# A hybrid decoder step on one core: the prompt's eight tiles in parts of 1, 2, 2, 2, 1 in place of 2, 2, 2, 2

## The reference, cut to what matters

```python
def layer(x, ...):
    n1 = rmsnorm(x, norm1_g)
    proj = n1 @ w_in          # q,k,v of attention; q,k,v,gates of GLA; merge gates ga, gb
    oa = banded_swa(qa, ka, va, attn_sinks)         # window of 128, 16 heads, 4 KV heads
    og, S_new = gla_recurrent(qg, kg, vg, log_a, S0, ...)   # state runs over the tokens, 4 heads
    og = rmsnorm(og, gla_norm_g) * silu(rb)
    u = sigmoid(ga) * oa + sigmoid(gb) * og
    x = x + u @ w_out
    return x + peer(rmsnorm(x, norm2_g), ...), new_k, new_v, S_new

def peer(h, ...):             # 8 heads, 16 experts each: 128 of 16384 experts for every token
    q = xk @ peer_wq          # 1024 -> 2048
    ... top 16 of 128 keys in two halves, top 16 of their sums, softmax -> eidx, g
    ue = take(peer_u, eidx)   # a row of 1024 floats for each token and expert
    act = gelu(sum(ue * xk))
    ve = take(peer_v, eidx)
    return sum(g * act * ve)
```

## Time and profile before

| | us |
|---|---|
| median of 3 runs (3849.88 to 3872.11) | 3852.84 |
| the profiled execution | 3859.83 |
| its span, first to last instruction | 3858.0 |
| indices of the first tile ready | 484.2 |
| indices of the first tile of parts 1, 2, 3 ready | 1216.0, 2165.3, 3010.2 |

### The profile page before, as it was taken

How to read it: one execution, slowest core, us unless ns; L and a number is a source line. 1 busy time by engine, 2 the same in 40 slices (tenths; PEclk the granted TensorE clock), 3 DMA queues, 4 the chain that set the end, 5 groups by cost and what they waited for, 6 DMA issues and landing times.

```text
span 3858.0 us, 33048 instructions
## 1 busy us (share of the span) xinstructions
PE 2894.0 (75%) x10008; PEld 1798.1 (47%) x10008; DVE 2808.5 (73%) x5630; ACT 731.2 (19%) x1677; POOL 2443.4 (63%) x2076
## 2 busy tenths in 40 slices
PE   8778689888687997887988768878777555555555
PEld 6667566456563665443664345545654111111111
DVE  0461797887788865866879897887879866667675
ACT  1321013332111131322111102322111110001001
POOL 0000077787667755765766777778667777777776
PEclk9889889899898997898999889989899777676677
DMA  4115399999999988898999999999999999999998
GB/s 149 54 36 183 110 376 407 350 356 396 420 403 345 405 331 324 306 328 309 396 402 375 326 363 403 401 328 370 421 411 380 338 371 368 363 377 385 367 400 336
DMA packets 342240, 1298.82 MB, mean 337 GB/s; under 512 B 39480, under 2 KB 48720, under 8 KB 321936
## 3 DMA queue, kind: packets, MB, share of 16 engines
q0 software_dynamic: 297216, 1082.26, 73.6%
q1 hardware_dynamic: 44848, 214.44, 14.3%
HBM read 1278.87 MB, written 19.76 MB: 337 GB/s over the span
## 4 chain that ended last, share of the span: by engine, by line
POOL 36%; PE 21%; DVE 14%; DMA 13%; issue 12%; DVEq 2%; ACT 0%; ACTq 0%; SPq 0%; POOLq 0%
POOL ringb L569 36%; DMA ringb<-in_v,eidx 9%; PE bank L834 8%; PE vsum L746 4%; DVE ringb L1294 4%; PE bank L1011 3%; DVE acc L1336 2%; PE bank L873 2%; PE bank L888 1%; DVE scT L1691 1%; PE bank L913 1%; DMA arena<-in_s 1%; DMA out_ss<-arena 1%; DMA ringb<-in_u,eidx 1%; DVE idx L1492 1%
## 5 line engine op out<-in xcount | busy, mean ns | idle before, releaser
L569 POOL DMA_INDIRECT ringb<-in_u,eidx x1024 | 1241.6, 1212 | 993.8 <-DVE eidx L1402 482.2
L746 PE MATMUL vsum<-ringb,diag 128*128 128x512 f32 x2160 | 1284.5, 737 | 646.6 <-DMA ringb<-in_v,eidx 603.8
L569 POOL DMA_INDIRECT ringb<-in_v,eidx x1024 | 1181.8, 1154 | 400.6 <-issue 300.1
L1294 DVE CUSTOM_DVE_ANT_0 ringb<-ringb,n2t 128x1024 f32<-128x1024 f32 x1032 | 1234.8, 1224 | 164.7 <-DMA ringb<-in_u,eidx 99.5
L746 PEld LDWEIGHTS vsum<-ringb,diag 128*128 128x128 f32 x2160 | 459.8, 228 | 1352.8 <-issue 1202.1
L1336 DVE SCALAR_TENSOR_TENSOR acc<-ringb,wgt,acc 128x1024 f32<-128x1024 f32 x484 | 622.3, 1286 | 326.0 <-DMA ringb<-in_v,eidx 313.7
L834 PE MATMUL bank<-wring,nTb 128*128 128x256 f32 x3024 | 683.4, 386 | 34.9 <-DMA wring<-in_w 31.1
L834 PEld LDWEIGHTS bank<-wring,nTb 128*128 128x128 f32 x3024 | 546.0, 182 | 175.5 <-DMA wring<-in_w 36.1
L1049 ACT ACTIVATE diag<-cst,wgt 128x128 f32<-128x128 f32 x540 | 206.9, 397 | 863.5 <-PE vsum L746 707.2
L873 PE MATMUL bank<-nTb,wring 128*128 128x256 f32 (+1 forms) x1152 | 264.0, 388 | 6.7 <-DMA wring<-in_w 4.1
L873 PEld LDWEIGHTS bank<-nTb,wring 128*128 128x128 f32 x1152 | 223.9, 195 | 60.6 <-issue 20.7
(11 more groups left out here) (231 smaller groups left out, 2212.5 us busy)
## 6 DMA issues: line engine op xcount, KB each, us to landing
wring<-in_w SPq DMA_DIRECT2D x152, 1024.0 KB, 7.8
ringb<-in_u,eidx POOLq DMA_INDIRECT x1024, 6.5
ringb<-in_v,eidx POOLq DMA_INDIRECT x1024, 6.6
n2t<-scratch_n SPq DMA_DIRECT2D x16, 512.0 KB, 7.4
oab<-in_xp SPq DMA_DIRECT2D x4, 1024.0 KB, 6.9
bTb<-in_keysT SPq DMA_DIRECT2D x4, 1024.0 KB, 9.1
vgb<-in_xp SPq DMA_DIRECT2D x4, 1024.0 KB, 8.9
scratch_h<-vgb SPq DMA_DIRECT2D x4, 1024.0 KB
```

Source lines behind the costliest of these rows:

```text
L569: pool.indirect_dma_start(out=ring[r], out_offset=None, in_=a["u"] if kind == "u" else a["v"], in_offset=bass.IndirectOffsetOnAxis(ap=at, ...
L746: last = mm(out[:, g * 512:(g + 1) * 512], lhs, ring[r][:, g * 512:(g + 1) * 512], start=(x == first), stop=(x == end))
L1294: v.tensor_tensor_reduce(out=ring[r], in0=ring[r], in1=n2t[:, n % 2, :], scale=1.0, scalar=0.0, op0=ALU.mult, op1=ALU.add, accum_out=dg[:, ...
```

## The change

One line changes:

```diff
-CH = (2, 2, 2, 2)
+CH = (1, 2, 2, 2, 1)
 NCH = len(CH)
 TM = max(CH)
 SC = 2
```

## The result

Over 16 runs each the changed kernel takes 3896.6 us (3872.7 to 3928.8) and the kernel before 3854.6 (3833.3 to 3881.1): a ratio of 1.012, with a 95% interval of 1.0095 to 1.0145. It is slower, by 42 us where 97 were forecast. The profiled execution has a span of 3891.7 us, 33.7 more than that of before.

The account below looks back on a forecast made before the run. After a head set by one mixer's chain, bytes of row gathers were taken to bound the kernel. 308 + 570 + 949 + 845 + 823 + 460 = 3955 us, 3950 on the median's scale (+2.5%), range 3870 to 4010.

Parts of the forecast that it names:

- The head: Start until the first expert indices are ready: one tile in place of two, 308 us in place of 484, -176.
- about 4.2: Head's feature blocks: us per weight unit with two buffers, a pair taking one load and one compute, 4.8 + 3.5 = 8.3.
- Stage 1: Two-tile mixer beside 56 quads in place of 120: 570 us in place of 732, -162, set by the mixer's chain.
- times 56/120: Stage 1: the some 264 us that 120 quads add to the mixer, scaled to 56 quads: 123, then taken as 102.
- Stage 2: Second two-tile mixer stage, with the sample: same mixer and number of quads, so unchanged at 949 us, give or take 15.
- Stage 4: New stage, one-tile mixer beside 128 quads with a fifth load of weights: 315 MB, 823 us.
- the price of a byte: Stage 4: transfers priced from stage 3's queues, 2.59 us per MB for gathers and 2.49 for SP's queue.
- The engines don't reach it: Stage 4: engines don't set its 823 us; DVE had 711 of 845 beside two tiles, and one tile less lowers that.
- the tail: Last stretch, gathers without a mixer: 460 us in place of 848, its row gathers setting the pace at 374 GB/s.
- stage 3: Third two-tile mixer stage: same mixer and number of quads, so unchanged at 845 us, give or take 15.
- Rival 1: Transfers have room left: stage 4 at 420 GB/s takes 750 us, 73 less, total 3877, +0.6%; chance 0.14.
- its own sign: Stage 4 running at 400 GB/s or over would mean that rival 1 holds; the forecast expected 375 to 390.

Follow-up runs that it names:

- parts 2, 2, 2, 1, 1: Kernel before with only its last two-tile part split into one-tile parts, head left at two tiles: 3935.7 us, ratio 1.022 against before.
- the run with short gathers and no gain: Changed kernel with four mixer PSUM banks and n2 read from PSUM throughout: ratio 1.010 against before; stage 4 took 800 us for 789.

## Why the prediction was right in direction and twice too large

**The head (-176 forecast, -170 measured) was right.** The weight ring shows in the feature blocks, PE's timeline in the head after (start, us, records, wait ahead):

```profile
29.44 7.47 PE L873 MATMUL bank<-nTb,wring 128*128 128x128 f32 x64 [1.34 <-DMA wring<-in_w]
38.18 7.41 PE L873 MATMUL bank<-nTb,wring 128*128 128x128 f32 x64 [1.28 <-DMA wring<-in_w]
46.81 3.39 PE L873 MATMUL bank<-nTb,wring 128*128 128x128 f32 x28 [1.21 <-DMA wring<-in_w]
```

A pair of units of 128 columns takes 8.7 us, of which 1.3 are a wait for the weights: 4.35 for "about 4.2" a unit.

**Stage 1 (570 forecast, 543 measured): the step "times 56/120" was too coarse.** Its four phases after, against the earlier trace rows:

```profile
314.00:403.00 89.00, 79.07 (x352) 66.18 (x352) 29.46 (x53) 13.59 (x30) 38.79 (x32) 0.93 0.79 301
403.00:517.00 114.00, 95.18 (x439) 71.38 (x439) 77.44 (x164) 45.32 (x118) 47.82 (x40) 0.88 0.65 225
517.00:725.00 208.00, 176.22 (x776) 138.23 (x775) 141.55 (x217) 47.14 (x84) 91.80 (x77) 0.96 0.81 286
725.00:857.00 132.00, 109.99 (x424) 77.00 (x424) 115.97 (x408) 18.29 (x45) 62.18 (x55) 0.92 0.83 304
```

The last of them begins with n2 on DVE, which in the head of the kernel before is at 381 us; so the same phases alone took 78, 103, 183 and 103 us. They are longer by 11, 11, 25 and 29 us, 75 in all with rounding; the forecast had 3, 19, 42 and 38. A quad's price isn't the mean of 120: 75 / 56 = 1.3 us here, 264 / 120 = 2.2 there. I had allowed for that in the features, where it was least needed, and hardly in GLA to wo. Why it is lower is argued from the rows: the first quads fall into waits that the engines have anyway, and the 732 us of stage 1 before were not the chain's price alone but also POOL's, 540 in gathers, 123 between them and 69 of waits.

**Stage 2 (949 forecast, 934 measured): "unchanged" forgot what POOL brings into it.** At 1216 us the kernel before was 11 gathers short of its mark, as the forecast itself worked out; after stage 1 of the change, with the ring full, POOL is 3 past it (203 for 4 x 56 - 24 = 200). So stage 2 has 502 gathers in place of 515: 13 x 1.4 = 18 us, an estimate. The five other runs on the change's parts took 926 to 935 us for it, the six on the parts of before with two tiles in stage 1 took 939 to 963.

**Stage 4 (823 forecast, 789 measured): the step that failed is the price of a byte, 2.5 us per MB, with nothing for the halved mixer ("The engines don't reach it").** A byte measured 0.9 for weights and 0.3 to 0.5 for rows, and halving the mixer beside nearly the same bytes gave 43 us (845 to 802, parts 2, 2, 2, 1, 1). The forecast reasoned that the tail has no mixer, DVE and PE are half idle and the rate is lower still, "so it is the row gathers that set the pace". They do, but in the tail by their number on POOL and not by their bytes: POOL had 335 us of gathers in 445 and 0.30 for each of 312 between them, 429 of 445. That sum stood in the rows and wasn't made. By POOL's ledger, stage 4 is stage 3 with 508 gathers for 524 (24 us), each of them 1.155 for 1.196 us (21 us), and 10 us less of waits for a buffer: 845 - 55 = 790. This is the same time written another way; that each part would have come off by itself isn't shown, and the run with short gathers and no gain says that it wouldn't. Rival 1 was nearer in the mechanism: the transfers had room (401 GB/s, its own sign), and how rows are used beside the gathers does lengthen them. Its 750 lies about as far below the 789 measured as 823 lies above. Its argument against itself, that the tail without a mixer is slower still, fails because there too DVE's products and sums lengthen the gathers.

**The signs named ahead.** First indices 314 (308 said), no second wait for indices, stage 1 DMA share 0.78, 1340 MB, POOL's wait for the first indices 171 less: as said. The fifth moment came at 3430 and not at 3495.

**The sum.** Stage 4 was priced 34 us too high, stage 1 27 and stage 2 15; the other three came 12 higher together. With rounding that is 3892 for 3955. The direction came out for the reasons given; that stage 3 and the tail came at their price was right too, and no luck: mixer, quads and rows are the same as before.

**Why it is slower at all.** The head gives 171 us. But the two tiles of part 1 still need their 468 us of chain, and only 56 quads can stand beside them; POOL waits there 255 us for 69. The 64 quads moved out of it are paid later at the tail's price, some 5.6 us each. The fifth set of weights costs some 32 us, by the run with an eighth of it.

## What to carry to other kernels

Draw up the ledger of every engine that issues transfers before reading a DMA share as a limit: instructions times duration plus the gap, against the stretch. Here it was 429 of 445 us, while a share of 0.97 stood for engines that were not full. A ledger says where the time lies, not what comes off when one item shrinks: in the tail shorter gathers gave 63 us, beside a mixer nearly nothing. A two-stage pipeline whose first step is made short to start the second earlier gains only if the next step has enough of the second's work beside it; a long step beside few rows leaves the issuing engine waiting.

## What the runs showed of the hardware that I had not expected

A gather of 128 rows costs POOL 0.94 us and 0.30 to the next, whether the rows have 4 or 2 KB. One that starts while a DVE instruction with two inputs in SBUF is running grows by what is left of that instruction less some 0.125 us, where that is 0.2 to 0.9 us; the longest such gather of the tail took 2.0 us, and its 536 gathers 591; with the U product's second input in PSUM only 2 of the 119 that start during one grow (524 us). One that starts with DVE idle doesn't grow, whatever begins after it: none of 385 in the whole kernel before, none of 392 in the changed one. POOL's smallest pace, 4.97 us a quad, and the highest rate seen beside a mixer, 420 GB/s, are nearly the same, so slices at 420 don't tell whether POOL or the transfers limit. With rows half as long the DMA share stayed at 0.65 for half the bytes. The same kernel before had medians from 3849 to 3904 us on different chips.
